# Sixteen bytes of padding behind each slot of two weight rings in a two-block transformer kernel

## The chip, the cores and the metric

One Trainium2 chip, one core of it. The metric is the device time of one execution in microseconds (us), the median of a few runs on the same chip; lower is better.

## The reference, cut to what matters

The program computes two small models one after the other on the same 256 tokens of 1024 features, all in float32: first a block with a gated recurrence, a short convolution and a retrieval layer over 16384 single-neuron experts, then two layers with SwiGLU feed-forward networks (2816 hidden features), a stick-breaking attention with pooling, and a block-sparse attention. Nearly all of the arithmetic is of one kind, activations of 256 tokens times a weight matrix:

```python
proj = h @ w_in[l]                                   # 1024 x 5632
q = (hf @ w_query).reshape(t, PEER_HEADS, 2, PEER_HALF)
...
act = jax.nn.gelu(jnp.einsum('thkd,td->thk', expert_u[ib], hb), approximate=False)
return jnp.einsum('thk,thkd->td', gb * act, expert_v[ib])
...
def swiglu(h, w_gate, w_up, w_down):
    return (jax.nn.silu(h @ w_gate) * (h @ w_up)) @ w_down   # four of these
...
proj = h @ w_in                                      # even_mixer
q, k, v = jnp.split(h @ w_qkv, 3, axis=-1)           # odd_mixer
```

The retrieval layer is computed densely: the gates of a token's experts are spread into a table G (256 tokens by 128 by 128 experts), all 16384 neurons are evaluated, and G picks the ones that count.

## The kernel before, in words

The weights come from HBM as one stream of 632 slabs (and 20 more that are loaded early), each 128 partitions by 1024 float32, so 4096 bytes in each partition, by one DMA on SyncE's queue. A slab goes through three rings of `RING = 4` slots in SBUF. It lands in `raw`. ScalarE (`split_hi`, L715) casts it to fp32r into the same slot of `w_hi`. VectorE (L1219) then subtracts: `w_lo = raw - w_hi`, again in fp32r (GpSimd does this for 16 slabs of one stage, L673). So a float32 weight is held as the sum of a high and a low part, each of which TensorE takes as fp32r in a single pass. The activations are split the same way, into `h_hi` and `h_lo` (together `h_parts`), `mid_hi` and `mid_lo`, `y_hi` and `y_lo`.

TensorE computes each product as three: high by high, high by low, low by high. All matmuls are issued through one helper (L2030), preceded by the load of 128 x 128 stationary values (LDWEIGHTS). Which operand is stationary differs:

- `project` (through `three`, L2037): a 128-column piece of a slab is stationary, 256 columns of `h_hi`, `h_lo` or `y_hi`, `y_lo` move. Output in `tile`. The same with `mid_hi`, `mid_lo` and output in `acc` for the down projections of the feed-forward networks.
- `wide` (L2060): a piece of `w_hi` is stationary and 512 columns (`h_hi` and `h_lo` of the same features) move, eight times; then a piece of `w_lo` is stationary and 256 columns of `h_hi` move, eight times. Output in `front`. This is the first half of each expert step and of each gate and up projection.
- the second half of each of the 128 expert steps (L2201): `mid_hi` or `mid_lo` is stationary, and 512 columns of a slot of `w_hi` or `w_lo` move, twelve times. Output in `acc`.
- `project_tokens` (L2120): `h_parts` is stationary, and 2 x 128 columns out of two neighbouring slots move.

The order of the work is written out by hand; semaphores hold the engines together. TensorE waits for `slab_lo_ready` before it takes a slab and counts `slab_used` after it; ScalarE waits for `slab_landed` and `slab_used`, VectorE for `slab_hi_ready`; SyncE loads into a slot of `raw` when `slab_lo_ready` says that it has been split.

All SBUF tensors are placed by hand, at `BASE + 4 * word` in each partition. `BASE` is 16512 = 129 x 128. Before, `raw` begins at word 0, `w_hi` at word 4096, `w_lo` at word 8192, `h_parts` at word 12288, the `mid` buffers at word 16384, all multiples of 32 words, and a slot has 1024 words: so each slot of each ring, each piece of 128 columns in it, `h_parts`, `scaled`, `hid` and `mid_*` begin at an address that is 0 modulo 128 bytes. `ARENA`, where most other tensors lie (x, the squares `sq`, `y_hi`, `y_lo`, `h_scaled`, `early_u`), begins at word 19592, which is 8 modulo 32; the offsets of these five in it keep that, so they begin at 32 modulo 128 bytes.

Of the kernel before, what the change touches and what calls it, by code (L numbers as in the profile page):

```python
# [24 lines left out]
F32R = mybir.dt.float32r  # L25
# [5 lines left out]
D = 1024  # L31
# [16 lines left out]
RING = 4  # L48
# [82 lines left out]


BASE = 16512
RAW, W_HI, W_LO = 0, RING * D, 2 * RING * D
H_HI = 3 * RING * D
H_LO = H_HI + KT * T
MID = H_LO + KT * T
COLS = MID + 5 * 2 * T
# [54 lines left out]
def build(nc, stream, x_in, cols_in, ones_in, keys_in, wpool_in, mixc_in, attc_in, out):  # L193
# [57 lines left out]
    with ExitStack() as ctx:  # L251
        def sb(name, at, shape, dt=F32):
            return nc.alloc_sbuf_tensor_at(name, [P] + shape, dt, offset=BASE + 4 * at)
# [2 lines left out]
            return ctx.enter_context(nc.semaphore(name))  # L256

        raw = sb("raw", RAW, [RING, D])
        w_hi = sb("w_hi", W_HI, [RING, D], F32R)
        w_lo = sb("w_lo", W_LO, [RING, D], F32R)  # L260
        h_parts = sb("h_parts", H_HI, [2, KT, T], F32R)
        assert H_LO == H_HI + KT * T
        h_hi, h_lo = h_parts[:, 0, :, :], h_parts[:, 1, :, :]
# [2458 lines left out]
```

## Time and profile before

| | us |
|---|---|
| median of 3 runs (2041.07 to 2041.62) | 2041.19 |
| span of the profiled execution, first to last instruction | 2039.6 |
| TensorE busy | 2005.6 (98%) |
| VectorE busy | 1508.3 (74%) |
| ScalarE busy | 1123.1 (55%) |
| GpSimd busy | 59.9 (3%) |

The profiled execution is known by its span; 1.6 us lie between it and the median. PE in the rows is TensorE's matmuls, PEld its loads of stationary values, DVE is VectorE, ACT is ScalarE, POOL is GpSimd. Matmuls are pipelined: the duration of one in a row (280 ns for 256 columns) is its latency, and the next starts long before it ends. What one costs is the distance between starts. It can be had from a merged row of the timeline, "start, length, xN": length less the duration of one, divided by N - 1; or from a window filled with matmuls of one kind: length of the window plus the duration of one, divided by the count.

### The profile page before, as it was taken

How to read it: one execution, taken by the hardware profiler on the slowest of the kernel's cores; microseconds unless marked ns; L12 is line 12 of the kernel's file. 1: busy time of each engine (PE TensorE's matmuls, PEld its weight loads, DVE VectorE, ACT ScalarE, POOL GpSimd, SP SyncE). 2: the span in 40 equal slices, each digit the busy share in tenths (PEclk: the TensorE clock that was granted, in tenths of full speed). 3: DMA queues.
4: the chain of work that ended last, by engine and by line, in shares of the span. 5: the costliest groups of instructions: out<-in, count | busy, mean ns of one | idle time of the engine just before them, and what ended most of it. 6: DMA issues, size and time to landing. Idle time of an engine off the chain costs nothing.

```text
span 2039.6 us, 37233 instructions
## 1 busy us (share of the span) xinstructions
PE 2005.6 (98%) x13232; PEld 1822.9 (89%) x13232; DVE 1508.3 (74%) x2564; ACT 1123.1 (55%) x1835; POOL 59.9 (3%) x40
## 2 busy tenths in 40 slices
PE   7999999999999999999999999999999999999998
PEld 6999999988888888888888999999999999999998
DVE  5868898877777777777777667776667667957666
ACT  5445537965555555555555555755555555655554
POOL 0000430000000000000000000000000000000000
PEclk9999999999999999999999999999999999999999
DMA  6445543055565666655665555455555555445553
GB/s 214 135 135 190 205 142 104 24 174 187 189 192 192 187 189 192 191 189 187 206 231 173 187 186 174 135 169 188 187 186 178 185 185 186 156 143 177 185 188 111
DMA packets 101466, 353.73 MB, mean 173 GB/s; under 512 B 11392, under 2 KB 16640, under 8 KB 101120
## 3 DMA queue, kind: packets, MB, share of 16 engines
q1 hardware_dynamic: 100944, 350.13, 52.5%
q10 hardware_dynamic: 432, 2.36, 0.3%
q8 instruction: 62, 1.02, 0.2%
q14 instruction: 28, 0.23, 0.0%
HBM read 348.77 MB, written 3.67 MB: 173 GB/s over the span
## 4 chain that ended last, share of the span: by engine, by line
PE 90%; DVE 7%; ACT 2%; issue 1%; DMA 0%; SPq 0%; DVEq 0%; ACTq 0%
PE front L2030 38%; PE acc L2030 35%; PE tile L2030 16%; DVE w_lo L1219 2%; ACT w_hi L715 1%; DVE rstd L1241 1%; ACT h_parts L741 0%; DMA raw<-stream 0%; PE front L2587 0%; DVE cand L1688 0%; DVE h_parts L1248 0%; DVE sq L1230 0%; DVE conv L1573 0%; DVE rest L1657 0%; DVE top_i L1653 0%
## 5 line engine op out<-in xcount | busy, mean ns | idle before, releaser
L1219 DVE TENSOR_TENSOR w_lo<-raw,w_hi 128x1024 fp32r<-128x1024 f32 x612 | 747.0, 1223 | 85.4 <-ACT w_hi L715 84.9
L715 ACT CAST w_hi<-raw 128x1024 fp32r<-128x1024 f32 x628 | 654.3, 1044 | 137.6 <-PE tile L2030 60.8
L2030 PE MATMUL front<-h_parts,w_hi 128*128 128x512 f32 (+1 forms) x2432 | 586.4, 377 | 4.2 <-ACT h_parts L741 2.5
L2030 PEld LDWEIGHTS front<-h_parts,w_hi 128*128 128x128 f32 x2432 | 436.5, 189 | 80.2 <-issue 2.4
L2030 PE MATMUL front<-h_parts,w_lo 128*128 128x256 f32 x2272 | 337.2, 282 | 0.0
L2030 PEld LDWEIGHTS front<-h_parts,w_lo 128*128 128x128 f32 x2272 | 318.8, 190 | 20.6
L2030 PE MATMUL tile<-h_parts,w_hi 128*128 128x256 f32 x1344 | 247.8, 286 | 5.1 <-DVE w_lo L1219 2.6
L2030 PEld LDWEIGHTS tile<-h_parts,w_hi 128*128 128x128 f32 x1344 | 209.5, 192 | 8.2 <-issue 4.9
L1304 DVE TENSOR_TENSOR scaled<-front,scaled 128x512 f32<-128x512 f32 x76 | 52.6, 692 | 215.1 <-ACT scaled L779 215.1
L2030 PE MATMUL acc<-w_hi,mid_hi 128*128 128x512 f32 x512 | 200.9, 392 | 2.1 <-DVE mid_lo L1793 1.7
L783 ACT ACTIVATE scaled<-scaled 128x256 f32<-128x256 f32 x188 | 78.6, 418 | 223.4 <-DVE scaled L1307 116.6
L2030 PE MATMUL acc<-w_hi,mid_lo 128*128 128x512 f32 x512 | 200.5, 392 | 0.0
L2030 PE MATMUL acc<-mid_hi,w_hi 128*128 128x256 f32 x704 | 199.2, 283 | 0.0
L2030 PE MATMUL acc<-mid_lo,w_hi 128*128 128x256 f32 x704 | 199.2, 283 | 0.0
L2030 PE MATMUL acc<-mid_hi,w_lo 128*128 128x256 f32 x704 | 199.2, 283 | 0.0
L2030 PE MATMUL acc<-w_lo,mid_hi 128*128 128x512 f32 x512 | 199.2, 389 | 0.0
L2030 PE MATMUL tile<-h_parts,w_lo 128*128 128x256 f32 x672 | 188.0, 283 | 0.0
L2030 PEld LDWEIGHTS acc<-mid_hi,w_hi 128*128 128x128 f32 x704 | 135.2, 192 | 0.0
L2030 PEld LDWEIGHTS acc<-mid_lo,w_hi 128*128 128x128 f32 x704 | 135.2, 192 | 0.0
L2030 PEld LDWEIGHTS acc<-mid_hi,w_lo 128*128 128x128 f32 x704 | 135.2, 192 | 0.0
L777 ACT COPY scaled<-front 128x256 f32<-128x256 f32 x108 | 40.2, 372 | 163.7 <-PE front L2030 163.6
L2030 PEld LDWEIGHTS tile<-h_parts,w_lo 128*128 128x128 f32 x672 | 128.7, 192 | 0.0
(324 smaller groups left out, 2519.5 us busy)
## 6 DMA issues: line engine op xcount, KB each, us to landing
raw<-stream SPq DMA_DIRECT2D x632, 512.0 KB, 3.7
early_u<-stream SPq DMA_DIRECT2D x20, 512.0 KB, 3.6
early_activations<-early_out SPq DMA_DIRECT2D x20, 128.0 KB, 3.5
scaled<-early_activations SPq DMA_DIRECT2D x10, 128.0 KB, 4.0
x<-x_t SPq DMA_DIRECT2D x2, 512.0 KB, 5.3
keysT<-keys_t ACTq DMA_DIRECT2D x1, 1024.0 KB, 6.3
attc<-attention_constants ACTq DMA_DIRECT2D x1, 1024.0 KB, 7.1
out_t<-h SPq DMA_DIRECT2D x4, 256.0 KB, 2.4
```

Source lines behind the costliest of these rows:

```text
L715: nc.scalar.copy(w_hi[:, s, :], raw[:, s, :]).then_inc(hi_ready, 1)
L777: nc.scalar.copy(scaled[:, k, 0:T], fronts[:, k, T:2 * T]).then_inc(lows_out, 1)
L783: nc.scalar.activation(scaled[:, k, 0:T], scaled[:, k, 0:T], func).then_inc(gate_ready, 1)
L1219: nc.vector.tensor_tensor(w_lo[:, s, :], raw[:, s, :], w_hi[:, s, :].bitcast(F32), ALU.subtract).then_inc(lo_ready, 1)
L1241: nc.vector.reciprocal(rstd[:, :], rstd[:, :]).then_inc(rstd_ready, 1)
L1304: nc.vector.tensor_tensor(to, fronts[:, :, 0:T], to, ALU.add).then_inc(parts_added, 1)
L2030: return nc.tensor.matmul(out, lhsT, rhs, start=start, stop=stop, **kw)
```

## The change

After each slot of `w_hi` and of `w_lo` come four unused words (16 bytes). A slot's 1024 words stay contiguous.

```diff
 BASE = 16512
-RAW, W_HI, W_LO = 0, RING * D, 2 * RING * D
-H_HI = 3 * RING * D
+SLOT = D + 4
+RAW, W_HI, W_LO = 0, RING * D, RING * D + RING * SLOT
+H_HI = W_LO + RING * SLOT
 H_LO = H_HI + KT * T
 MID = H_LO + KT * T
...
         raw = sb("raw", RAW, [RING, D])
-        w_hi = sb("w_hi", W_HI, [RING, D], F32R)
-        w_lo = sb("w_lo", W_LO, [RING, D], F32R)
+        w_hi = sb("w_hi", W_HI, [RING, SLOT], F32R)[:, :, 0:D]
+        w_lo = sb("w_lo", W_LO, [RING, SLOT], F32R)[:, :, 0:D]
```

The slots of `w_hi` now begin at 0, 16, 32 and 48 modulo 128 bytes, those of `w_lo` at 64, 80, 96 and 112. `raw` stays at 0. `H_HI` and all that is placed after it move up by 32 words, 128 bytes, and keep their place modulo 128. No instruction, wait, loop or transfer is added, taken out or moved; the 2 x 128 columns that `project_tokens` takes from two slots now lie 4112 instead of 4096 bytes apart.

## Rows read from the trace of the kernel before

**Rows 1.** The page, part 1 (busy time and instructions) and TensorE's granted clock in 40 slices
```profile
PE 2005.6 (98%) x13232; PEld 1822.9 (89%) x13232; DVE 1508.3 (74%) x2564; ACT 1123.1 (55%) x1835; POOL 59.9 (3%) x40
...
PEclk9999999999999999999999999999999999999999
```
**Rows 2.** The page, part 4: the chain that ended last, by line
```profile
PE front L2030 38%; PE acc L2030 35%; PE tile L2030 16%; DVE w_lo L1219 2%; ACT w_hi L715 1%; DVE rstd L1241 1%; ACT h_parts L741 0%; DMA raw<-stream 0%; PE front L2587 0%; DVE cand L1688 0%; DVE h_parts L1248 0%; DVE sq L1230 0%; DVE conv L1573 0%; DVE rest L1657 0%; DVE top_i L1653 0%
```
**Rows 3.** Groups by form, whole span: count, busy us, mean ns of one, idle before
```profile
L2030 PE MATMUL front<-h_parts,w_hi 128*128 128x512 f32 x2112 | 526.6, 391 | 1.6 <-DVE scaled L1362 1.5
...
L2030 PE MATMUL front<-h_parts,w_lo 128*128 128x256 f32 x2272 | 337.2, 282 | 0.0
...
L2030 PE MATMUL tile<-h_parts,w_hi 128*128 128x256 f32 x1344 | 247.8, 286 | 5.1 <-DVE w_lo L1219 2.6 <-ACT h_parts L741 2.0 <-DVE kk L1271 0.5
...
L2030 PE MATMUL acc<-w_hi,mid_hi 128*128 128x512 f32 x512 | 200.9, 392 | 2.1 <-DVE mid_lo L1793 1.7 <-DVE mid_lo L1330 0.5
L2030 PE MATMUL acc<-w_hi,mid_lo 128*128 128x512 f32 x512 | 200.5, 392 | 0.0
L2030 PE MATMUL acc<-mid_hi,w_hi 128*128 128x256 f32 x704 | 199.2, 283 | 0.0
L2030 PE MATMUL acc<-mid_lo,w_hi 128*128 128x256 f32 x704 | 199.2, 283 | 0.0
L2030 PE MATMUL acc<-mid_hi,w_lo 128*128 128x256 f32 x704 | 199.2, 283 | 0.0
L2030 PE MATMUL acc<-w_lo,mid_hi 128*128 128x512 f32 x512 | 199.2, 389 | 0.0
L2030 PE MATMUL tile<-h_parts,w_lo 128*128 128x256 f32 x672 | 188.0, 283 | 0.0
...
L2030 PE MATMUL front<-h_parts,w_hi 128*128 128x256 f32 x320 | 59.8, 287 | 2.5 <-ACT h_parts L741 2.5
```
**Rows 4.** Timeline of PE in two expert steps: start us, length us, what, count
```profile
601.67 1.98 PE L2030 MATMUL front<-h_parts,w_hi 128*128 128x512 f32 x8
```
**Rows 5.** The same view, about 400 us later
```profile
1001.40 2.00 PE L2030 MATMUL front<-h_parts,w_hi 128*128 128x512 f32 x8
1003.24 1.12 PE L2030 MATMUL front<-h_parts,w_lo 128*128 128x256 f32 x8
...
1004.42 0.40 PE L2030 MATMUL acc<-w_hi,mid_lo 128*128 128x512 f32 x1
1004.66 0.39 PE L2030 MATMUL acc<-w_lo,mid_hi 128*128 128x512 f32 x1
```
**Rows 6.** Windows, matmuls into `tile` alone: first over h_parts, then three over y
```profile
34.00:53.00 19.00, 19.00 (x160) 1.00 0.77 244
...
176.00:194.00 18.00, 18.00 (x156) 1.00 0.56 186
...
1817.50:1825.50 8.00, 8.00 (x71) 1.00 0.50 157
...
1333.00:1345.00 12.00, 12.00 (x104) 1.00 0.49 158
```
**Rows 7.** Groups by form, whole span: two-input DVE and one-input ACT over 1024 columns
```profile
L1219 DVE TENSOR_TENSOR w_lo<-raw,w_hi 128x1024 fp32r<-128x1024 f32 x612 | 747.0, 1223 | 85.4 <-ACT w_hi L715 84.9
L715 ACT CAST w_hi<-raw 128x1024 fp32r<-128x1024 f32 x628 | 654.3, 1044 | 137.6 <-PE tile L2030 60.8 <-PE front L2030 58.6 <-PE acc L2030 14.1
...
L1230 DVE TENSOR_TENSOR sq<-sq 128x1024 f32<-128x1024 f32 x8 | 9.8, 1222 | 3.0 <-ACT sq L734 1.6 <-ACT sq L857 1.4
...
L734 ACT ACTIVATE sq<-x 128x1024 f32<-128x1024 f32 x7 | 7.3, 1045 | 0.0
```
**Rows 8.** Windows of all engines, a stretch of expert steps: PE, PEld, DVE, ACT, POOL
```profile
600.00:800.00 200.00, 200.00 (x1017) 170.83 (x1016) 151.51 (x218) 108.67 (x182) 0.00 (x0) 1.00 0.61 190
```
**Rows 9.** Timeline of PE in the early experts, plain float32 operands
```profile
286.69 2.10 PE L2030 MATMUL acc<-h_scaled,early_u 128*128 128x256 f32 x9
```

## Prediction

> **What bounds the kernel now.** I read the page first: TensorE is busy for 2005.6 of 2039.6 us, at the full granted clock in every slice [rows 1]. Then the chain that ended last, by line: matmuls hold 38 + 35 + 16 = 89% of it, and the two splitting lines, L1219 and L715, 3% [rows 2]. So time is won or lost in what one matmul costs, and hardly anywhere else. The groups by form say which matmuls those are [rows 3]. Those that read a weight ring, in their larger groups, are: with 512 moving columns 2112 + 3 x 512 = 3648, and with 256 moving columns 2272 + 1344 + 3 x 704 + 672 + 320 = 6720.
>
> What one costs is read from distances between starts. Eight matmuls of 512 columns take 1.98 us in one expert step [rows 4], so (1.98 - 0.39) / 7 = 0.227 us each; in another 2.00 us, so 0.230 us each, and eight of 256 columns take 1.12 us, so (1.12 - 0.28) / 7 = 0.120 us each [rows 5]. The granted clock is full, so 2.4 GHz, at which 256 columns are 106.7 ns and 512 columns 213.3 ns. Both sizes thus pay the same 13 to 14 ns on top, a little over 30 cycles, whatever their length. It is this surcharge that the change could touch; over all 10,368 matmuls it is some 140 us.
>
> Does it depend on addresses? The kernel holds one natural comparison. In `project`, with a weight piece stationary at 0 modulo 128 bytes, either `h_parts` moves (also at 0) or `y_hi`/`y_lo` (at 32). Windows filled with nothing else give, over h, (19.00 + 0.28) / 160 = 120.5 ns; over y, (18.00 + 0.28) / 156 = 117.2, (8.00 + 0.28) / 71 = 116.6 and (12.00 + 0.28) / 104 = 118.1 ns, mean 117.3 [rows 6]. Same line, same shapes, same engine order; what differs is where the moving operand lies. Against the 120.0 of an undisturbed run that is 2.7 ns less. It is the one piece of evidence in this trace that placement modulo 128 matters to TensorE; it could also be placement on a coarser scale, since y is in another part of memory.
>
> **The change part by part.** *Instructions, waits, DMAs.* None is added or removed, and `raw`, the only DMA target of the stream, stays where it is: 0 us.
>
> *Splitting, L715 and L1219.* They now write, and L1219 also reads, at 16 to 112 modulo 128 while `raw` stays at 0. Today all operands are at 0: 1044 and 1223 ns. The same shapes on x and sq, which lie at 32 modulo 128, take 1045 and 1222 ns [rows 7]. So the absolute place is worth 1 ns. No row has operands at different places modulo 128 in one such instruction. Bounds: -5% and +5%, that is 0.06 us on each slab; in the expert steps VectorE is busy for 151.5 of 200 us and ScalarE for 108.7 [rows 8], so that much stays beside TensorE, which hides it. Where L1219 and L715 are on the chain (3% of the span, some 60 us), 5% is 3 us either way. I take 0. The 16 slabs of GpSimd go with them.
>
> *Matmuls of 256 columns.* I take the step seen between h and y, 2.7 ns, for every one whose weight slot leaves 0 modulo 128. High slots are used twice for each use of a low slot; one of four high slots stays at 0, so 2/3 x 1/4 = 1/6 keep their cost. 6720 x 5/6 x 2.7 ns = 15.1 us less. Bounds: no change (0), and the whole surcharge gone (13.3 ns, 89 us). I take the value near the bottom since it alone has been seen.
>
> *Matmuls of 512 columns.* No row has them with operands at different places. They run at 227 ns in a settled run [rows 4] and at 230 ns over the eight that follow a run of 256 columns, single distances reaching 1004.66 - 1004.42 = 0.24 us [rows 5]. So out of step they get dearer, not cheaper, as far as the trace goes. Bounds: the 2.7 ns of the short ones (-9.8 us), and every one at 0.235 us or a little more against about 229 ns now (+6 x 3648 = +22 us). I take 0, between the two.
>
> *Sum.* -15.1 us on TensorE, of which 89% lies on the chain: -13.5 us. From 2039.6 of the profile that is 2026.1 us, and with the 1.6 us between span and median 2027.7, in round numbers 2027. If TensorE gets this much faster, nothing else becomes the bound: 13.5 us spread over 2040 is under 1%, and VectorE has a quarter of the expert steps free [rows 8].
>
> **Rivals.** *A: placement is nothing to TensorE, and h and y differ for another reason.* For it: y lies in another part of memory and is read in other stages, so its place modulo 128 is not the only difference. Against it: the distances over y were under those over h in all three stages [rows 6]. Time: 2041. The Trainium skill, SBUF — State Buffer, section "Who interferes with whom", says that TensorE has two independent read ports, one for the moving operand and one for the stationary, and that only the port pair shared by VectorE and GpSimd contends. By that rule no placement in SBUF changes a matmul, and the time would be 2041. The trace speaks against it with 117.3 against 120.5 ns.
>
> *B: the surcharge is a collision between moving reads and the load of stationary values, and different places remove most of it.* For it: it is the same for 256 and 512 columns, and so is the load that runs beside each; the plain float32 matmuls of the early experts, of which 256 columns take (2.10 - 0.38) / 8 = 215 ns, stand only 2 ns above the 213.3 ns that 512 cycles are at 2.4 GHz [rows 9]. Against it: y is 32 bytes off and regains 2.7 of 13.3 ns only. With all of it, 11.3 ns less on 10,368 matmuls is 117 us, 89% of it 105: 1936 us; with half of it 1989. The Trainium skill, TensorE: Matmul & The Clock Gate, section "Back-to-back issue gap", gives 2.5 ns over the columns as the gap between matmuls. By it there would be 109.2 and 215.8 ns to reach, hence (10.8 x 6720 + 13.2 x 3648) ns, 121 us, at 89% 108 us, an estimate of 1933 us.
>
> *C, the other side: moving stream and stationary load are held in a steady step by their equal places, and this is good for the long ones.* Every slab, and in the second half of an expert step every third matmul, then changes the relation of the two addresses, so that the 512-column matmuls stay in the state that they are now in only after a change of size [rows 5]. At 0.235 us each that is +22 us, at 89% +20: 2061; if the short ones keep their 15.1 us, it is 2047. It decides from a mean rise of 4.1 ns on the 3648 long ones (4.1 x 3648 = 15.1 us), or of 1.3 ns, where the short ones gain nothing, to be seen at all. For it: the settled run of eight is the cheaper one, 227 against 230 ns [rows 4, 5]. Against it: the short ones are dearest where all places are equal [rows 6].
>
> **How the numbers follow.** A measurement of this kernel can tell about 0.2%, 4 us, from no change. The forecast (some gain on the short ones, the long ones within 3 ns of today) 0.42, its own range 2008 to 2036; A 0.21 at 2041; B, half or all of it, 0.13 at 1936 to 1989; C 0.24 at 2045 to 2061. Faster by over 0.2%: 0.42 + 0.13, 0.55; within: 0.20; slower: 0.25. The range for 8 in 10 leaves out the deeper part of B and the far end of C: 1968 to 2052.
>
> **What would show it.** Right: eight 256-column matmuls of `front<-h_parts,w_lo` in about 1.10 us instead of 1.12, windows over h_parts at 117 to 118 ns, and different values for different slots, the steps of a ring of four. The 512-column run x8 at 1.97 to 2.01 us. L1219 and L715 at 1223 and 1044 ns within 1%; the same 13,232 matmuls. Wrong: 120.0 ns everywhere (A); 110 to 115 ns (B); runs of 512 columns above 2.03 us (C); or L1219 above 1280 ns, with PE waiting for it. The forecast fails first if y's advantage comes from something other than its place modulo 128.

## The result: slower by 0.3%, and the profile after

| | before | after |
|---|---|---|
| median, us | 2041.13 (8 runs, 2040.64 to 2041.62) | 2047.31 (8 runs, 2046.15 to 2048.24) |
| ratio | | 1.003, 95% interval 1.0021 to 1.0038 |
| span of the profiled execution | 2039.6 | 2046.4 |

Forecast was 2027, faster; measured is 6 us more than before. The interval lies clear of 1. The page of the kernel after shows nothing new in kind: the same instructions, TensorE just as full.

```profile
PE 2012.1 (98%) x13232; PEld 1815.6 (89%) x13232; DVE 1507.4 (74%) x2564; ACT 1121.5 (55%) x1835; POOL 59.8 (3%) x40
```

TensorE is busy for 6.5 us more, with the same 13,232 matmuls [rows 1]; VectorE and ScalarE are not slower. The groups by form, whole span, answer to [rows 7]; the matmuls of 512 columns answer to [rows 3].

```profile
L1220 DVE TENSOR_TENSOR w_lo<-raw,w_hi 128x1024 fp32r<-128x1024 f32 x612 | 746.7, 1222 | 84.2 <-ACT w_hi L716 83.8
L716 ACT CAST w_hi<-raw 128x1024 fp32r<-128x1024 f32 x628 | 652.8, 1042 | 135.3 <-PE tile L2031 59.6 <-PE front L2031 57.9 <-PE acc L2031 14.0
L2031 PE MATMUL front<-h_parts,w_hi 128*128 128x512 f32 x2112 | 534.5, 395 | 1.8 <-DVE scaled L1363 1.6
L2031 PE MATMUL front<-h_parts,w_lo 128*128 128x256 f32 x2272 | 334.3, 279 | 0.0
```

The split takes 1222 and 1042 ns, as before. The long matmuls hold 534.5 us against 526.6, the short ones of `front` 334.3 against 337.2. The timeline of an expert step in the kernel after, with [rows 4, 5] to compare (start, length, what, count):

```profile
602.28 2.02 PE L2031 MATMUL front<-h_parts,w_hi 128*128 128x512 f32 x8
604.13 1.12 PE L2031 MATMUL front<-h_parts,w_lo 128*128 128x256 f32 x8
605.08 0.39 PE L2031 MATMUL acc<-w_hi,mid_hi 128*128 128x512 f32 x1
...
605.77 0.39 PE L2031 MATMUL acc<-w_hi,mid_hi 128*128 128x512 f32 x1
```

Eight long ones now take 2.02 us, (2.02 - 0.39) / 7 = 233 ns each, where they took 227 or 230; three in the second half 0.69 us, 230 each. The windows say the same for a stretch of expert steps (all engines, as in [rows 8]): 1002 matmuls in 200 us, before 1017.

```profile
600.00:800.00 200.00, 200.00 (x1002) 168.09 (x1001) 149.93 (x216) 107.17 (x180) 0.00 (x0) 1.00 0.59 188
```

And over y, where the kernel before was cheap, it is now dearer: (18.00 + 0.28) / 154 = 118.7 ns against 117.2 [rows 6].

```profile
176.00:194.00 18.00, 18.00 (x154) 1.00 0.58 198
```

Where the time went, by the start of the same matmul in both traces: number 3000 starts at 398.5 us before and 396.8 after (a gain of 1.7 us while nearly all are short ones), number 7000, behind the experts, at 1163.5 and 1170.7 (a loss of 8.9 us while nearly two in three are long), number 13,195, the last before the closing ones of 2 columns, at 2027.9 and 2033.1 (1.9 us back in the feed-forward layers, where short ones prevail again), and number 13,231, the very last, at 2033.8 and 2040.6.

The 1.6 us lost at the very end are a matter of the clock and not of operands. Windows over the 32 closing matmuls of 2 columns, first the kernel before, then two of the kernel after (TensorE busy, count, granted clock, DMA share, GB/s):

```profile
2028.30:2032.00 3.70, 3.70 (x32) 1.00 0.01 2
```

```profile
2033.57:2035.10 1.53, 1.53 (x14) 1.00 0.01 5
2035.50:2038.82 3.32, 3.32 (x16) 0.50 0.00 0
```

All 32 take 3.70 us at the full clock before, and 5.25 us after, since the granted clock fell to its lower level, 1.2 GHz, when about half of them had started; until then TensorE was busy all but without a break, for 3.42 of the 3.50 us from 2030.00 and all of the 1.53 us above. In the kernel before it fell only behind the 32. The eight times after lie in two groups, four at 2046.2 to 2046.5 us (mean granted clock 0.998) and four at 2048.1 to 2048.2 (0.996 or 0.997, the profiled one among them), and so do those of two kernels below (medians 2047.3 and 2048.2), so that 1 us between such medians says nothing; that the earlier fall of the clock makes the groups is likely and not shown.

For all kernels below I give the mean distance between the starts of neighbouring matmuls that read a ring, over those of 512 columns (distances of 215 to 260 ns, some 3636) and of 256 columns (105 to 135 ns, some 7640). They come from the one profiled execution of each kernel, the times from all of its executions. That table is the thread of the experiments:

| kernel | long, ns | short, ns | time, us | ratio to before, 95% |
|---|---|---|---|---|
| before | 228.7 | 119.5 | 2041.1 to 2041.5 | |
| after | 232.3 | 118.4 | 2047.3 | 1.003 (1.0021 to 1.0038) |
| padding of 128 bytes | 232.9 | 118.9 | 2053.2 | 1.006 (1.0043 to 1.0076) |
| high ring alone (low ring unpadded, moved by 128) | 231.3 | 118.6 | 2044.8 | 1.0018 (1.0008 to 1.0028) |
| low ring alone | 232.2 | 118.2 | 2045.9 | 1.0024 (1.0014 to 1.0033) |
| no padding, rest moved by 128 | 232.2 | 118.5 | 2047.3 | 1.0029 (1.0018 to 1.004) |
| no padding, rest moved by 256 | 228.7 | 119.5 | 2041.3 | 1.0001 (0.9991 to 1.001) |
| padding, rest moved by 256 | 232.5 | 118.2 | 2048.2 | 1.0031 (1.0019 to 1.0044) |
| h_parts alone at 64 | 230.6 | 118.0 | 2041.0 | 0.9999 (0.999 to 1.0008) |
| h_parts alone at 112 | 230.1 | 116.9 | 2034.2 | 0.9966 (0.9952 to 0.9979) |
| the same, mid of the networks at 112 too | 229.8 | 115.5 | 2022.4 | 0.9908 (0.9893 to 0.9923) |

The change in two terms: (232.3 - 228.7) x 3636 = +13.1 us and (118.4 - 119.5) x 7640 = -8.4 us, together +4.7 of the 6.8 us between the spans. Another 1.6 us are the closing matmuls at the lower clock. The rest, half a microsecond on balance, in distances outside these limits and in waits, I have not taken apart.

### The profile page after: what moved, and what is told of

The parts are those of the page before. It is cut to its first block, busy times and chain, and to the rows that moved or that the text cites. A ratio compares the mean times of both kernels' runs of the same rounds, so it can differ in the third digit from the quotient of the medians.

```text
span 2046.4 us, 37233 instructions
## 1 busy us (share of the span) xinstructions
PE 2012.1 (98%) x13232; PEld 1815.6 (89%) x13232; DVE 1507.4 (74%) x2564; ACT 1121.5 (55%) x1835; POOL 59.8 (3%) x40
## 4 chain that ended last, share of the span: by engine, by line
PE 86%; DVE 9%; ACT 3%; issue 1%; DMA 0%; SPq 0%; DVEq 0%; ACTq 0%
PE front L2031 38%; PE acc L2031 34%; PE tile L2031 13%; DVE w_lo L1220 3%; ACT w_hi L716 1%; DVE rstd L1242 1%; DVE S L1530 0%; ACT h_parts L742 0%; PE front L2588 0%; DMA raw<-stream 0%; DVE h_parts L1249 0%; DVE x L1409 0%; DVE sq L1231 0%; DVE cand L1689 0%; DVE win L1889 0%
## 5 line engine op out<-in xcount | busy, mean ns | idle before, releaser
L1220 DVE TENSOR_TENSOR w_lo<-raw,w_hi 128x1024 fp32r<-128x1024 f32 x612 | 746.7, 1222 | 84.2 <-ACT w_hi L716 83.8
L716 ACT CAST w_hi<-raw 128x1024 fp32r<-128x1024 f32 x628 | 652.8, 1042 | 135.3 <-PE tile L2031 59.6
L2031 PE MATMUL front<-h_parts,w_hi 128*128 128x512 f32 (+1 forms) x2432 | 593.6, 380 | 4.2 <-ACT h_parts L742 2.1
L2031 PE MATMUL front<-h_parts,w_lo 128*128 128x256 f32 x2272 | 334.3, 279 | 0.0
```

The costliest lines, as they stand in the source:

```text
L716: nc.scalar.copy(w_hi[:, s, :], raw[:, s, :]).then_inc(hi_ready, 1)
L1220: nc.vector.tensor_tensor(w_lo[:, s, :], raw[:, s, :], w_hi[:, s, :].bitcast(F32), ALU.subtract).then_inc(lo_ready, 1)
L2031: return nc.tensor.matmul(out, lhsT, rhs, start=start, stop=stop, **kw)
```

## The experiments

**Placement by itself.** This kernel leaves the whole computation out and ran once: runs of 40 matmuls for each pair of places, then the kernel's own sequences, all other engines idle while they run.

```diff
+for n in (256, 512):
+    for p in range(0, 128, 16):
+        RUNS.append((0, [p], n, P))      # moving at 0, stationary at p
+    for p in range(16, 128, 16):
+        RUNS.append((p, [0], n, P))      # moving at p, stationary at 0
...
+    RUNS.append((0, [0], n, 64))         # 64 stationary columns
```

> This kernel leaves the whole computation out and times runs of fp32r matmuls with nothing beside them: 40 in a row for each pair of places modulo 128 bytes of the moving and the stationary operand, at 256 and 512 columns, then the kernel's own sequences for slots at 0, 16, 32, 48 with low parts at 64 more. Theory P (the relation of the two places modulo 128 sets the surcharge): the distance depends on the difference of the places, equal places (0/0, 16/16, 32/32, 64/64) give 120 and 227 ns, a difference of 32 gives 117 ns at 256 columns, and at 512 columns different places give 229 to 236 ns, so more than equal ones. Copies of the operand at the same place modulo 128 elsewhere in memory give the same. Rival S (spacing or coarser placement, not the place modulo 128): all runs give 120 and 227 ns, or the two copies differ. Rival W (the writers on the other engines cause the 230 ns): here, with idle writers, 512 columns take 227 ns everywhere. With 64 or 32 stationary columns in place of 128 the surcharge of 13 ns halves or quarters if the load of the stationary values causes it, and stays if not.

The timeline of that kernel; m and w name the moving and the stationary tensor with its place modulo 128. `m0b` and `w0b` are 42240 bytes apart, 165 x 256; `m0xb` is a copy of `m0b` 4224 bytes on, so at the same place modulo 128, but 128 modulo 256 away from `w0b`.

```profile
89.88 4.83 PE L103 MATMUL bank<-m64b,w0b 128*128 128x256 f32 x40 [0.26 <-DVE tick L84]
...
162.83 9.37 PE L103 MATMUL bank<-m0b,w0b 128*128 128x512 f32 x40 [0.26 <-DVE tick L84]
172.45 9.60 PE L103 MATMUL bank<-m0b,w16b 128*128 128x512 f32 x40 [0.26 <-DVE tick L84]
...
270.59 9.59 PE L103 MATMUL bank<-m64b,w0b 128*128 128x512 f32 x40 [0.26 <-DVE tick L84]
...
319.60 9.35 PE L103 MATMUL bank<-m32b,w32b 128*128 128x512 f32 x40 [0.26 <-DVE tick L84]
...
368.20 9.57 PE L103 MATMUL bank<-m0xb,w0b 128*128 128x512 f32 x40 [0.26 <-DVE tick L84]
```

Rival W fell: with nothing beside them, the long ones take (9.60 - 0.39) / 39 = 236 ns in most cases and (9.37 - 0.39) / 39 = 230 at equal places, the slow first one included. Theory P fell too: `m0xb` costs 5 ns more than `m0b` although both are at 0 modulo 128. Over the last distances of each run, when they have settled, the long ones stand at 226.7 ns for 0/0 and 32/32, which are equal modulo 256, and otherwise at 230 to 234, but for 0/4 and 0/112, which come to 226.7 as well; 16/16, equal too, stands at 231.1. The short ones stand at 120 ns for 0/0, 32/32, 0/16 and 80/0, at 113.3 for 64/0 and 112/0, and between 115.6 and 118.8 for the rest. (These names, moving/stationary, are modulo 128. Modulo 256 `w4b` lies at 132 and `w112b` at 240, `m16b` and `w16b` both at 144, `m64b` at 192 and `w64b` at 64.) So equality modulo 256 is a good place for the long ones, but neither the only one nor a sure one. And the surcharge does not follow the size of the stationary load in any order: with 64 and 32 stationary columns in place of 128, at 0/0, the long runs go from 226.7 to 230.3 and 231.7 ns, the short ones from 120.0 to 113.3 and 117.8.

Two more things stand in this trace. In the kernel's own sequence with all places equal, the first long ones after eight short ones come at distances of 233, 236, 228, 233 and 230 or 231 ns before they settle at 226.7. Eight of them make 2.00 us, the length of the run in [rows 5], so that it needs no other engine. And the place modulo 256 does not fix the settled distance. 64/0 and 0/64 lie equally far apart, 192 modulo 256 from the stationary to the moving operand, and settle at 113.3 and 117.8 ns. Even the same two tensors can settle at either value: eight short ones of `m0b` over `w64b` stand at 117.7 ns in each of three repeats when long ones over `w0b` went before (the row below, start and length of all eight), and at 113.3 ns in each of three repeats when long ones over `w64b` went before. What ran before is a second condition besides the places.

```profile
461.29 1.10 PE L110 MATMUL bank<-m0b,w64b 128*128 128x256 f32 x8
```

**Padding of 128 bytes, all places modulo 128 as before.** (The last slot of each ring goes without, for room. The edit is shown against the kernel after.)

```diff
-SLOT = D + 4
-RAW, W_HI, W_LO = 0, RING * D, RING * D + RING * SLOT
-H_HI = W_LO + RING * SLOT
+SLOT = D + 32
+RAW, W_HI, W_LO = 0, RING * D, RING * D + RING * SLOT - 32
+H_HI = W_LO + RING * SLOT - 32
```

> Padding of 128 bytes in place of 16: slots and all that follows move, but every place modulo 128 is as before the change. Theory P: 2041 us, settled distances of 120 and 227 ns are back. Rival S (the spacing of 4096 bytes between slots was good, or the shift of everything behind the rings costs): 2047 us as with 16 bytes.

2053.2 us, slower still than the change, where 2041 or 2047 had been expected: neither came. Places modulo 128 are not what counts, since they did not move. Modulo 256 they did: the slots of both rings alternate between 0 and 128. Long ones 232.9 ns, short ones 118.9; against the change that is 0.6 x 3636 + 0.5 x 7640 = 6.0 us. The closing matmuls, which the clock slows by 1.6 us in the change, run at the full clock here, and the rest of 4.4 us is nearly the 4.6 us between the spans (2051.0 and 2046.4).

**One ring at a time.**

```diff
-RAW, W_HI, W_LO = 0, RING * D, 2 * RING * D
-H_HI = 3 * RING * D
+SLOT = D + 4
+RAW, W_HI, W_LO = 0, RING * D, RING * D + RING * SLOT + 16     # e3_high_only: w_lo keeps slots of D words
+H_HI = W_LO + RING * D
...
+RAW, W_HI, W_LO = 0, RING * D, 2 * RING * D + 16               # e4_low_only: w_hi keeps slots of D words
+H_HI = W_LO + RING * SLOT
```

> Only the high ring is padded (places 0, 16, 32, 48), the low ring stays at 0. Theory P: the long matmuls over the high ring still rise by some 2 to 3 ns, the short ones over high slots fall by about 1 ns; 2043 to 2047 us. Rival S: half of the added time, about 2044. If the change of place between high and low part is what unsettles (and not the place itself), distances are as after the change, 2047.

> Only the low ring is moved and padded (places 64, 80, 96, 112), the high ring stays at 0. Theory P: runs of eight long matmuls over the high ring settle at 227 ns again, the sequences high, high, low in the second half of an expert step do not; the short ones over low slots fall by 1 to 3 ns; 2036 to 2042 us. Rival S: about 2044. If any change of place unsettles, the expert steps stay at 5.57 us and the time is 2045 to 2047.

2044.8 and 2045.9 us. The first is what theory P and rival S both allowed; the second lies outside the 2036 to 2042 of theory P. For the second I had expected the long runs over the unmoved high ring to settle again; the matmuls of 512 columns over the high ring in `front` take 233.0 ns in the mean, and 231.2 in the other kernel. But in both kernels h_parts and what follows had also moved by 128 bytes, as in the change, and in the first the low ring too, so these two do not separate the rings cleanly. That led to the next pair.

**No padding at all, only the side effect of the change: everything behind the rings moved.**

```diff
-H_HI = 3 * RING * D
+H_HI = 3 * RING * D + 32     # e5_shift128: 128 bytes; e6_shift256: + 64, 256 bytes
```

> No padding in the rings; only h_parts, mid and all that lies behind them move up by 128 bytes, the side effect of the change. Every place modulo 128 is that of the kernel before. Theory M (what counts is the difference of the two places modulo 256; equal modulo 256 settles at 227 ns for 512 columns and 120 ns for 256): 512 columns at about 232 ns, 256 columns at about 119 ns, together 2045 to 2050 us. Rival P (places modulo 128): 2041 us, distances of 120 and 227 ns.

> The same with 256 bytes. Theory M: all as before, 2041 us, distances of 120.0 and 226.7 ns. Rival (any departure from the old spacing, a multiple of 4096, costs): 2045 us or more.

128 bytes: 2047.3 us, all of the loss without a byte of padding. 256 bytes: 2041.3 us, and distances equal to those before within 0.1 ns. The first eight long ones of an expert step in each, timeline, first the kernel moved by 128, then the one moved by 256:

```profile
603.23 2.02 PE L2030 MATMUL front<-h_parts,w_hi 128*128 128x512 f32 x8
```

```profile
606.75 1.98 PE L2030 MATMUL front<-h_parts,w_hi 128*128 128x512 f32 x8
```

2.02 against 1.98 us. The windows of 200 us over expert steps hold 1004 and 1017 matmuls, again first the kernel moved by 128:

```profile
600.00:800.00 200.00, 200.00 (x1004) 168.56 (x1003) 149.42 (x215) 107.53 (x180) 0.00 (x0) 1.00 0.59 189
```

```profile
600.00:800.00 200.00, 200.00 (x1017) 170.82 (x1016) 151.33 (x218) 109.11 (x183) 0.00 (x0) 1.00 0.60 190
```

Shown by this pair: what counts repeats after 256 bytes and not after 128. Theory M takes it for the place of the two operands to each other. That is not shown: the rings stayed in both kernels, so the absolute place of the activations modulo 256 would explain the pair as well. Of the runs of 40, 32/32 with the same two distances as 0/0 speaks for the relation, and 16/16, with others, against.

**The padding without the side effect.** (Against the kernel after.)

```diff
-H_HI = W_LO + RING * SLOT
+H_HI = W_LO + RING * SLOT + 32     # activations 256 bytes on, equal modulo 256 to slot 0 of w_hi
```

> The change with its padding, but h_parts, mid and the rest moved by 256 instead of 128 bytes, so that modulo 256 they are equal to the slot at 0 again. Theory M, by the sequences of the first experiment: 512 columns dearer by 1 to 3 ns than before, 256 columns cheaper by 2 ns; 2039 to 2044 us, less than the change's 2047. Rival P: the same as the change, 2047 us.

2048.2 us. Missed: I had expected less than the change. The padding alone costs as much as the side effect alone, and both together no more than either. In all three kernels the long ones stand at 232.2 to 232.5 ns in the mean, where they had 228.7.

**A grid of places, the kernel's own sequences, nothing beside them.**

```diff
+CASES = [(0, 0, l) for l in range(0, 256, 16)]          # activations, w_hi, w_lo
+CASES += [(0, 16, 80), (0, 32, 96), (0, 48, 112)]
+CASES += [(128, 0, 64), (128, 16, 80), (128, 32, 96), (128, 48, 112), (128, 0, 0)]
+CASES += [(0, 128, 0), (0, 128, 128), (0, 64, 64), (64, 0, 0)]
```

This kernel and the second grid below leave the whole computation out, and ran once each.

> Leaves the whole computation out. The kernel's three sequences of matmuls (eight of 512 columns over w_hi and eight of 256 over w_lo; twelve of 512 with the slots moving; 256 columns in the order high, high, low) with nothing beside them, for the place of w_lo in steps of 16 over 256 bytes, for the four slots of the change with activations at 0 and at 128 modulo 256, and for a few more. Theory M: equal places give 120.0 and 226.7 ns in the steady part; activations at 128 with slots as in the change give long distances of 230 to 234 ns, and the sum over the kernel's counts reproduces its +6 us; some place of w_lo gives 113 to 118 ns on the short ones while w_hi stays equal and the long ones of the first sequence keep 227. Rival P: cases that are equal modulo 128 but not modulo 256 give the same distances.

Mean distances from the starts in its trace, ns (twelve long ones with the slots moving; short ones in the order high, high, low): 0, 0, 0 gives 226.7 and 120.0; the four slots of the change, activations at 128, give 231.1, 232.7, 235.6, 230.4 and 116.7, 117.7, 120.0, 117.2; 128, 0, 0 gives 232.5 and 118.7, although equal modulo 128. Rival P fell for good. The case 0, 64, 64 gave 228.8 and 113.3. So in these two sequences the old placement was the best of the cases for the long ones and, with one other, the worst for the short ones: the two kinds want different places. In the first sequence it was not the best: eight long ones after eight short ones over equal places stand at 230.1 ns in the mean, and at 228.4 when only the slot of `w_lo`, which the long ones do not read, lies at 80 or 208 instead of 0. That is again what ran before, and no place of the long ones' own operands. Whether the distances of the grid add up to the 6 us of the kernel, as was expected, is not worked out here.

**Using it: h_parts off by 64 and by 112, mid left equal.**

```diff
-H_HI = 3 * RING * D
-MID = H_LO + KT * T
+H_HI = 3 * RING * D + 16     # e9_h64: 64 bytes
+MID = H_LO + KT * T + 48     # and back to 256 in all
...
+        h_parts = sb("h_parts", H_HI, [2 * KT * T + 4], F32R)[:, 4:].rearrange(   # e11_h112: H_HI + 24, MID + 40
+            "p (a k t) -> p a k t", a=2, k=KT)
```

> No padding; h_parts alone moves to 64 modulo 256, everything behind it moves by 256 and stays equal to the slots modulo 256. Theory M, by the grid (case 64, 0, 0: a slab of eight long and eight short ones in 2756 ns against 2796 for 0, 0, 0; three short ones over h at 117.8 against 120.0): 40 ns on each of some 300 slabs and 2.2 ns on some 2400 short ones, together 17 us on TensorE, 15 of them on the chain: 2026 us, 2024 to 2034. The second halves of the expert steps and the down projections stay as before (229 and 120 ns). Rival E (equality modulo 256 is the only good placement, any departure costs about 6 us, as the last three did): 2045 us or more.

> Leaves the whole computation out. Whole expert steps (eight long and eight short over h, then twelve long with mid stationary at 0) for the place of h_parts in steps of 16 over 256 bytes, then a few places of w_lo beside h at 64 and 192. Theory M: 64 is cheaper than 0 by 40 ns in a step, 128 dearer, and the curve is irregular, since the pattern of settling decides and not a distance; theory P would give a curve that repeats after 128 bytes.

> No padding; h_parts alone at 112 modulo 256, everything behind it moved by 256 in all. Theory M, by the second grid (case 112, 0, 0: an expert step in 5500 ns against 5513 for 0, 0, 0, and 113.3 against 120.0 ns for the short ones in the order high, high, low): 13 ns on 108 steps, 16 ns on 176 gate and up slabs, 6.7 ns on some 2000 short ones, together 17 us, 16 of them on the chain: 2025 us. The grid missed 2041 for h at 64 by 15 us, since patterns in a run without neighbours last longer than in the kernel; so 2025 to 2041. Rival E (equality modulo 256 cannot be beaten): 2041 or more.

At 64: 2041.0 us, no difference, a clear miss. The short ones over h fell from 119.5 to 117.2 ns, as theory M says, but the long ones of `front` rose from 228.8 to 231.6 ns and ate it. The second grid, whole expert steps in one run, agrees with the kernel where the first had not: 5547 ns with h at 64 against 5513 at 0. So a step is dearer by 34 ns where 40 ns less had been expected of it, too. And the short ones in the order high, high, low settle at 113.3 ns there, where the case 64, 0, 0 of the first grid, with the same places modulo 256, had 117.8. It also shows a curve with no order that I can name (5513 at 0, 5534, 5547, 5580 at 16, 32, 48, 5500 at 112, 5580 at 128, 5520 at 192) and 113.3 ns on the short ones at 64, 112 and 192. The curve does not repeat after 128 bytes, as theory P would have it. At 112: 2034.2 us, faster by 0.34%, within the expected 2025 to 2041 but 9 us short of the sum. TensorE's busy time fell by 12.8 us, from 2005.6 to 1992.8, and the span by 7.4, from 2039.6 to 2032.2: the time in which TensorE is idle rose from 34.0 to 39.4 us.

**And the mid buffers of the feed-forward networks, which move 256 columns at a time, off by 112 as well; those of the experts, which are stationary under long ones, stay.**

```diff
+        ffn_hi = sb("ffn_hi", MID + 6 * T + 24, [2 * T + 4], F32R)[:, 4:].rearrange("p (a t) -> p a t", a=2)
+        ffn_lo = sb("ffn_lo", MID + 8 * T + 24, [2 * T + 4], F32R)[:, 4:].rearrange("p (a t) -> p a t", a=2)
...
-                        ins = three(acc[:, m, :], n % RING, m * P, mid_hi[:, s % 2, :], mid_lo[:, s % 2, :],
+                        ins = three(acc[:, m, :], n % RING, m * P, ffn_hi[:, s % 2, :], ffn_lo[:, s % 2, :],
```

> As before, and the mid_hi and mid_lo of the feed-forward networks (not those of the expert steps) lie at 112 modulo 256 too, so that their 2112 short matmuls move from a place that is 112 off the slots. Theory M: these fall from 120.0 to between 113 and 118 ns, 4 to 14 us less than the kernel without this, 2012 to 2037 us. Rival E: no less than the other, 2041 or more.

2022.4 us, 0.92% faster than the kernel before and 1.2% faster than the change. The short ones that move mid fell from 119.5 ns in the kernel with h_parts alone at 112 to 114.3, 2112 x 5.2 = 11.0 us, and the time by 11.8 between these two. The timeline of a down projection in the kernel with both: three matmuls in 0.34 us, so 113 ns each.

```profile
1404.53 0.28 PE L2032 MATMUL acc<-ffn_hi,w_hi 128*128 128x256 f32 x1
...
1404.87 0.28 PE L2032 MATMUL acc<-ffn_hi,w_hi 128*128 128x256 f32 x1
```

The same place in the kernel before, 0.36 us for three:

```profile
1405.22 0.28 PE L2030 MATMUL acc<-mid_hi,w_hi 128*128 128x256 f32 x1
...
1405.58 0.28 PE L2030 MATMUL acc<-mid_hi,w_hi 128*128 128x256 f32 x1
```

## Why the prediction was wrong

*What bounds the kernel.* Right. 4.7 of the 6.8 us between the spans are in the distances between matmuls over the rings, and 1.6 us in the closing matmuls at the lower clock. That the clock is full in every slice was read off too coarsely: a digit 9 stands for 90% or more, and in the last 7 us of the kernel before the granted clock is at its lower level. The remark that nothing else becomes the bound if TensorE gets faster could not be tested by the change; with h_parts at 112 a gain of 12.8 us on TensorE gave 7.4 us of span, so it did not hold there.

*Instructions, splitting.* Right: 1222 and 1042 ns for 1223 and 1044, same counts. Splitting was taken as 0 and is 0.

*Matmuls of 256 columns.* Right in sign, too large: 2.7 ns on five in six was forecast, 15.1 us; 1.1 ns on all, 8.4 us, was measured. The comparison of h with y was sound, but a step seen for one pair of places (32 apart) is not the step for others: in the runs of 40 the settled distance of the short ones lies anywhere from 113.3 to 120.1 ns.

*Matmuls of 512 columns.* This is the step that failed. "I take 0, between the two" was wrong: +3.6 ns, 13.1 us, more than the gain on the short ones. The trace had said so: the only rows with long ones out of step showed 230 ns in a run and single distances of 0.24 us, and I had no row that showed them cheaper than the settled 227 ns. Between two bounds of which one had rows behind it and the other was carried over from another size, the value belonged on the side of the rows. With +13.1 us in place of 0 the same sum gives 2039, and with the measured 1.1 on the short ones 2045.

*The displacement by 128 bytes.* I wrote down that all that lies behind the rings keeps its place modulo 128 and took it for nothing. It was not even a term in the sum. Alone it costs 6.0 us. I counted places modulo 128; in this kernel a move by 128 bytes changed the distances and a move by 256 did not.

*Rivals.* C came nearest, in time (2045 to 2061, measured 2047.3) and in half of its mechanism: equal places hold the long ones in a steady step, and losing that costs more than it brings on the short ones. It laid this to the places of the slots modulo 128 alone, and so it missed that the displacement of the activations does it without any padding. That its 2047 was met owes something to luck: it stands on +22 and -15.1 us, where +13.1 and -8.4 were measured. It had 0.24. A fell: placement does matter, and the two read ports of TensorE which the Trainium skill (SBUF — State Buffer, "Who interferes with whom") calls independent do not make it indifferent, by 2047.3 against 2041.3 us for two displacements of otherwise equal kernels. B fell for this change, which left the short ones at 118.4 ns and made the long ones dearer. Other places do remove half of the surcharge of the short ones (113.3 ns), and none tried takes the settled long ones under 226.7. The 2.5 ns of the Trainium skill (TensorE: Matmul & The Clock Gate, "Back-to-back issue gap") would give 109.2 and 215.8; the section gives that figure for an isolated matmul and says that a stream of loads and matmuls goes by other ones, which the prediction left out. The surcharge did not shrink in step with the stationary load, as a collision with that load would let one expect: 64 columns gave 113.3 ns on the short ones, but 32 gave 117.8, and the long ones rose with both.

*What was said would show it.* Eight short ones of `front` in about 1.10 us: 1.12 in the row shown, 1.09 to 1.12 over the whole kernel, where they had 1.11 or 1.12. The run of eight long ones "at 1.97 to 2.01 us": 2.02 in the row shown; over the whole kernel 62 of 264 such runs keep within 2.01 us, and before the change 258 did. The sign named for C, above 2.03 us, was set too far out: most of them stand at 2.02 and 2.03, and the loss was there all the same.

## What to carry to other kernels

A kernel bound by fp32r matmuls, like this one, pays a surcharge on each that depends on where the two operands lie and on what ran just before; it can be read as the distance between starts less columns at the granted clock, and it is worth a look for each size of matmul separately, since in runs without change of size the best place for one size was among the worst for the other. A move of all activations by 256 bytes changed nothing here and one by 128 cost 6 us, so try whole multiples of 256 if nothing is to change, and count every tensor that a new size pushes along as part of the change. Where a term has rows on one side only, take the value from that side.

## What was not expected of the hardware

- Distances lock. With operands equal modulo 256 they are 120.0 and 226.7 ns, 13.3 above 256 and 512 columns at 2.4 GHz. Off that, most go through repeating patterns (236, 231, 236, 231 with the slots 64 away in the single runs). Over all places tried the settled means lie between 226.7 and 235.6 ns for the long and, with h at 4 bytes in the second grid as the dearest, between 113.3 and 123.3 ns for the short. In the kernel moved by 128 bytes the means are 232.2 and 118.5.
- Plain float32 operands do not show it. In the early experts 256 columns take 216.3 ns in the kernel before, in the one after and in the one moved by 128 bytes. The third and fourth slab of the program are taken straight from `raw`, which stayed, by activations that moved by 128 bytes: 32 matmuls of 256 columns in 7.17 us in both kernels. Timeline of the kernel before, then of the one after:

```profile
19.59 7.17 PE L2030 MATMUL tile<-h,raw 128*128 128x256 f32 x32 [0.22 <-DVE kk L1271]
```

```profile
17.65 7.17 PE L2031 MATMUL tile<-h,raw 128*128 128x256 f32 x32 [0.22 <-DVE kk L1272]
```

- What inside TensorE or SBUF produces the pattern is open. It is not the writing of the other engines, which were idle in the single runs, and the size of the stationary load moves it without order. That 16/16 did not lock and 0/112 did, and that the same pair stood at 117.7 or 113.3 ns by what ran before, says that the difference modulo 256 is not the whole rule. It is also open why the padding and the displacement, each of which costs 6 to 7 us, cost no more together.
